# Eight convolution blocks and all of z multiplied from high and low weight halves, with memory's keys and values parked in DRAM, on one Trainium2 core

## The chip, the core and the metric

The kernel runs on one core of a Trainium2 chip. The core has five engines, each with its own in-order instruction stream: PE (TensorE, the matrix engine), DVE (VectorE), ACT (ScalarE), POOL (GpSimd) and SP (SyncE, which here only issues DMAs). They wait for each other through semaphores. The metric is the device time of one execution in microseconds (us); lower is better.

## What is computed

One step of a one-layer hybrid decoder on 320 tokens (256 of a prompt, 64 of eight samples), in 32-bit floats. Cut to the part that the change touches:

```python
def token_mixer(hn, ...):                   # hn: 320 tokens x 1024
    proj = hn @ w_in                        # z 1024, xbc 1536, dt 16, u5 1024, gates 2 x 1024
    z, xbc, dt_raw, u5, gate_a, gate_b = jnp.split(proj, IN_PROJ_SPLITS, axis=-1)
    xbc_c, new_conv = causal_depthwise_conv(xbc, conv_buf, conv_w, conv_b)   # 4 taps, then silu
    xs, bm, cm = jnp.split(xbc_c, [...], axis=-1)
    dt = softplus(dt_raw + ssd_dt_bias)
    y_ssd, new_ssd = ssd_chunked_scan(xh, dt, a, bm, cm, ssd_h0)             # 16 heads
    y_ssd = rms_norm((y_ssd + ssd_d * xh) * silu(z), ssd_norm_g)
    ...                                     # S5 branch, GLU, gates, w_mix_out
def memory_kv(mem, g, w_k, w_v):            # mem: 256 x 1024, keys and values are outputs too
    mn = rms_norm(mem, g)
    return mn @ w_k, mn @ w_v
...                                         # attention over memory, then 32 experts (192 MB of weights)
```

## The kernel before

The program has two parts. In the first some 650 us everything up to the experts' router is computed; PE is the busy engine. Then the experts' weights stream in, 1 MB chunks through a ring of places in on-chip memory, and DMA is busy without a break until near the end.

**Products.** A projection of 1024 inputs to 128 outputs for 320 tokens is one "job": eight matmuls of a stationary 128x128 tile of weights with a moving 128x320 tile of the normed input. `proj` (line 1310) does this on plain 32-bit floats; the profile shows each such matmul as two records. `proj_split` (lines 1667 to 1669) does it from halves: weights and input are each split into a high half (the value rounded to the reduced type that TensorE takes in fewer passes) and a low half (what is left), and three products are summed, high x high, high x low, low x high; each is one record. From job `ga0` on all projections are made this way, on "units" of 256 weight columns: ACT writes the high half (line 1006), DVE the low half (line 2419).

**Order.** `plan()` lists all jobs in the order in which PE does them, and gives each in turn one of six PSUM banks. PE waits with a job until the bank's job of six places earlier has been emptied. Every engine's stream is written out by hand in the same order of jobs, so what an engine waits for also holds back all that stands behind it. The stages that matter here:

- `STAGE`: memory's keys `mk0..7` (to `kT`) and values `mv0..3` (to `vm`), with the S5 branch's inputs between them. DVE runs the S5 scans (`scan`, `step_out`) meanwhile.
- `xbc0..11`, the convolution's input. For each, ACT copies the bank to a padded row `cvin` (`conv_in`, lines 878 and 879), DVE does the four taps into `cvout` (`conv`, lines 2222 to 2229), and ACT applies silu two blocks later (`conv_silu`, lines 885 and 888). `cvin` and `cvout` have two places each: `conv_in(m)` waits for `conv(m-2)`, and `conv(m)` waits for `conv_silu(m-2)`. The small jobs `dtT`, `dt3`, `cs` (time steps and their sums) stand after `xbc5`, `xbc7`, `xbc9`.
- `ye/yo/kk/fy/ty`, the S5 branch's outputs: `kk0` (line 1480) gives taps that DVE spreads to `kbd` (lines 2322 and 2330), `fy` (line 1491) uses them, `ty` needs ACT to have emptied `ye` and `yo`.
- `ko..`: the keys transposed back (line 1295) for their output; then `z0`, `z1`, `z2` by `proj` with small jobs between; `cumT`, `ecs`, `tr/tb/cb`.
- the heads: eight rounds t = 0..7 (`cs`, `yi`, `h0`, `yx`, `ns`). The five jobs `z3..7` are spread over it matmul by matmul (`rest_z`, line 1565): eight ahead of it, three in each round, eight behind it; then `hl`, then `ga0`.

**Weights.** Blocks of 512 columns (2 MB) go through two slots (`load_block`, line 532). SP loads a block when the last job of the block two before it is done: the second block of `xbc` when `mv3` is done, the third when `xbc3` is, the first of z (`z0..3`) when `xbc7` is, the second of z (`z4..7`) when `xbc11` is.

**Stores.** POOL issues them: values (`out_mv`, line 749) after `mv3`, keys (`out_mk`, line 751) after `ko`.

## Time and profile before

| what | value |
|---|---|
| median of three runs | 1124.7 us (1123.86 to 1130.07) |
| the profiled execution | 1127.23 us, of which its span is 1125.5 us |
| PE, DVE, ACT, POOL busy | 87%, 41%, 27%, 5% of the span |
| DMA | 297.69 MB, mean 265 GB/s |

The profile's page cuts the span in 40 slices of 28 us and gives each engine's busy tenths. Timeline rows give start, duration, engine, line, what is written from what, its size and how many instructions are merged; in brackets the idle time before it and who ended that. The duration of a merged row runs from its first start to its last end, and a matmul's end is modelled and overlaps the next one's start; so the time that a matmul costs is read from start to start. A row for a line alone may end with "DMA to landing", the time from a transfer's issue to its completion.

### The profile page before, as it was taken

The numbers are of one execution on the slowest core, as the hardware profiler recorded it, in microseconds if no ns is written. First come the engines' busy times: TensorE is split into PE (matmuls) and PEld (weight loads), VectorE is DVE, ScalarE is ACT, GpSimd is POOL, SyncE is SP. The second block draws the span as 40 slices with busy tenths as digits, with TensorE's granted clock in tenths as the row PEclk, the third lists the DMA queues.
The fourth block names the chain that finished last, engine by engine and source line by source line (L and its number), as shares of the span: only waits on it lengthen the run. The fifth ranks groups of instructions, "written<-read, shape, count | busy, mean of one in ns | idle before, by whom it ended". The sixth has DMA issues, their size and how long they took to land.

```text
span 1125.5 us, 15894 instructions
## 1 busy us (share of the span) xinstructions
PE 980.3 (87%) x6619; PEld 655.0 (58%) x6619; DVE 464.4 (41%) x795; ACT 305.3 (27%) x610; POOL 53.9 (5%) x82
## 2 busy tenths in 40 slices
PE   6999999999999999999898999976867768787575
PEld 4788467886779999999766954432222313232121
DVE  5999965405676554555455331020202020201014
ACT  4142124235546435544443341000000000000002
POOL 2602300010110000000000000000000000000000
PEclk9999999999999999999999999988898888788778
DMA  9581433023436574523578749999999999999994
GB/s 272 120 231 61 149 142 137 14 85 119 136 105 228 183 266 150 197 88 130 214 287 344 305 158 409 422 421 422 422 421 422 422 420 422 423 421 422 422 418 150
DMA packets 92435, 297.69 MB, mean 265 GB/s; under 512 B 21053, under 2 KB 31001, under 8 KB 68172
## 3 DMA queue, kind: packets, MB, share of 16 engines
q1 hardware_dynamic: 89812, 288.81, 67.0%
q0 software_dynamic: 2112, 7.28, 2.0%
q8 instruction: 53, 0.87, 0.3%
q10 hardware_dynamic: 440, 0.59, 0.2%
q14 instruction: 18, 0.15, 0.0%
HBM read 286.76 MB, written 9.90 MB: 264 GB/s over the span
## 4 chain that ended last, share of the span: by engine, by line
PE 61%; SPq 29%; DVE 4%; DMA 2%; issue 2%; ACT 1%; POOL 1%; DVEq 0%; ACTq 0%; POOLq 0%
SPq L629 29%; PE bank L1310 11%; PE bank L1295 6%; PE bank L1667 5%; PE bank L1668 5%; PE bank L1669 5%; PE bank L1954 3%; PE bank L1319 2%; DMA ring<-in_w_exp_down_dram 2%; PE bank L2003 2%; PE bank L1678 2%; PE bank L1565 2%; PE bank L1680 2%; PE bank L1679 2%; PE bank L1491 2%
## 5 line engine op out<-in xcount | busy, mean ns | idle before, releaser
L1954 PE MATMUL bank<-ring,work 128*32 128x512 f32 x704 | 134.9, 698 | 39.2 <-DMA ring<-in_w_exp_gate_dram 21.9
L1310 PE MATMUL bank<-work,ring 128*128 128x320 f32 (+1 forms) x480 | 125.6, 420 | 0.0
L1667 PE MATMUL bank<-ops,usplit 128*128 128x320 f32 x368 | 114.3, 311 | 1.1 <-DVE usplit L2419 1.1
L1668 PE MATMUL bank<-ops,usplit 128*128 128x320 f32 x368 | 114.0, 310 | 0.0
L1669 PE MATMUL bank<-ops,usplit 128*128 128x320 f32 x368 | 113.9, 310 | 0.0
L1310 PEld LDWEIGHTS bank<-work,ring 128*128 128x128 f32 x480 | 90.1, 190 | 30.7 <-issue 1.0
L1970 PE MATMUL bank<-ring,work 128*32 128x512 f32 x352 | 73.0, 822 | 39.0 <-DMA ring<-in_w_exp_down_dram 29.8
L1954 PE MATMUL bank<-work 128*32 128x512 f32 x256 | 87.1, 714 | 12.4 <-DMA work<-in_w_exp_up_dram 6.6
L2419 DVE TENSOR_TENSOR usplit<-ring,usplit 128x2048 fp32r<-128x2048 f32 x32 | 73.3, 2291 | 58.5 <-ACT usplit L1006 58.5
L1954 PEld LDWEIGHTS bank<-ring,work 128*32 128x32 f32 x704 | 32.4, 125 | 106.2 <-issue 86.9
L1006 ACT ACTIVATE usplit<-ring 128x2048 fp32r<-128x2048 f32 x32 | 61.4, 1919 | 52.7 <-PE bank L1669 36.7
L2718 DVE TENSOR_TENSOR work<-bank,g 128x512 f32<-128x512 f32 x8 | 5.5, 692 | 161.6 <-PE bank L2003 161.6
L1667 PEld LDWEIGHTS bank<-ops,usplit 128*128 128x128 f32 x368 | 69.2, 188 | 2.2 <-issue 2.0
L1669 PEld LDWEIGHTS bank<-ops,usplit 128*128 128x128 f32 x368 | 69.2, 188 | 0.0
L1668 PEld LDWEIGHTS bank<-ops,usplit 128*128 128x128 f32 x368 | 69.1, 188 | 0.1
L2003 PE MATMUL bank<-work 128*128 128x128 f32 (+1 forms) x384 | 68.7, 308 | 0.2 <-DVE work L2662 0.2
L2003 PEld LDWEIGHTS bank<-work 128*128 128x128 f32 (+1 forms) x384 | 52.3, 188 | 27.1 <-issue 13.3
L1970 PEld LDWEIGHTS bank<-ring,work 128*32 128x32 f32 x352 | 17.0, 145 | 82.0 <-issue 54.9
L2733 DVE COPY work<-bank 128x512 f32<-128x512 f32 x8 | 5.5, 692 | 124.0 <-PE bank L1970 124.0
L1678 PE MATMUL bank<-usplit,ops 128*128 128x256 f32 (+1 forms) x192 | 54.6, 285 | 1.7 <-DVE ops L2424 1.0
L1680 PE MATMUL bank<-usplit,ops 128*128 128x256 f32 (+1 forms) x192 | 53.9, 281 | 0.0
L1679 PE MATMUL bank<-usplit,ops 128*128 128x256 f32 (+1 forms) x192 | 53.9, 281 | 0.0
(461 smaller groups left out, 1555.7 us busy)
## 6 DMA issues: line engine op xcount, KB each, us to landing
ring<-in_w_exp_up_dram SPq DMA_DIRECT2D x45, 1024.0 KB, 26.1
ring<-in_w_exp_gate_dram SPq DMA_DIRECT2D x43, 1024.0 KB, 26.1
ring<-in_w_exp_down_dram SPq DMA_DIRECT2D x43, 1024.0 KB, 26.4
ring<-in_w_in_dram SPq DMA_DIRECT2D x11, 2048.0 KB, 8.8
work<-in_w_exp_gate_dram SPq DMA_DIRECT2D x16, 1024.0 KB, 21.7
work<-in_w_exp_up_dram SPq DMA_DIRECT2D x16, 1024.0 KB, 26.3
work<-in_w_exp_down_dram SPq DMA_DIRECT2D x14, 1024.0 KB, 26.7
ring<-in_w_glu_dram SPq DMA_DIRECT2D x4, 2048.0 KB, 8.7
```

The lines of the kernel that those rows point to most:

```text
L629: sp.dma_start(v, src).then_inc(sem_, 16)
L1310: ins = nc.tensor.matmul(b[:, 0:N], wv[:, k, P * (m % 4):P * (m % 4 + 1)], src[:, k, 0:N], start=(k == 0), stop=(k == KT - 1))
L1667: nc.tensor.matmul(b[:, 0:T], wh, hi_[:, k], start=(k == 0), stop=False)
L1668: nc.tensor.matmul(b[:, 0:T], wh, lo_[:, k], start=False, stop=False)
L1669: ins = nc.tensor.matmul(b[:, 0:T], wl, hi_[:, k], start=False, stop=(k == KT - 1))
L1678: nc.tensor.matmul(b[0:R, 0:256], th_, uhi[u % 2][:, k], start=(k == 0), stop=False)
L1679: nc.tensor.matmul(b[0:R, 0:256], th_, ulo[u % 2][:, k], start=False, stop=False)
L1680: ins = nc.tensor.matmul(b[0:R, 0:256], tl_, uhi[u % 2][:, k], start=False, stop=(k == KT - 1))
L1954: ins = nc.tensor.matmul(psum[part][ES * x:ES * (x + 1), :], xs[i % 2][:, kk, x], wt[x][:, k], start=(kk == 0), stop=(kk == KT - 1))
L1970: ins = nc.tensor.matmul(psum[2 + n_][ES * x:ES * (x + 1), :], hhT[:, j, x], wd[x][:, k, BLK * n_:BLK * (n_ + 1)], start=(j == 0), stop=(j ...
L2003: ins = nc.tensor.matmul(b[:, P * j:P * (j + 1)], tn[0:R, c, 4 * r_ + j], sel[i % 2][0:R, c].rearrange("p x n -> p (x n)"), start=(c == 0) ...
L2419: TT(ulo[u % 2], unit_raw(u), uhi[u % 2].bitcast(F32), ALU.subtract).then_inc(s["wlo"], 1)
```

## The change

- **Halves.** `xbc4..11` and `z0..7`, sixteen jobs, are multiplied as three products of halves. `HALVED` lists them in order, two halves (of four 128x128 tiles) each. ACT writes high half i to one of three places in `w_his` (`high_half`), when the products of half i-3 are done and the weight block is in; DVE writes the low half over the weights in their slot (`low_half`); `half_products` on PE waits for it. The four jobs `xbc0..3` (`WHOLE`) stay as they were.
- **z spread anew.** `z0`, `z1`, `z2` now stand between `xbc8`, `xbc9`, `xbc10` and `xbc11`; `z3` is made where it was; `z4..7` go as four pieces (each three matmuls) into each of the eight rounds of heads, and none is left behind them. `cs` moves from after `xbc9` to after `xbc11`.
- **The input's halves.** `hn_hi`, `hn_lo` are made before the convolution and no more at `ga0`. They and `w_his` lie where keys, values and `kout` were. So the `ko` jobs move between `mv0` and `mv1`; POOL stores keys and values and parks a copy of both in DRAM (`kv_scratch`, 1 MB each); ACT waits for the keys' store ahead of `hn_hi`, DVE for the values' store and copy ahead of `hn_lo`. After `gb7` POOL loads both back, and the attention waits for that.
- **Moves.** `cvin`, `cvout` and `dtS` lie where the memory input was; `ecs`, `btok`, `cbT`, `zT` have other places; `conv` of a block is interleaved with low halves on DVE, and three low halves (22 to 24) stand behind six `block_taps`; `hl` stands after `ga0`; unit 0's low half stands in the last round of heads; the silu of z is in two pieces.

When a block of weights is loaded is as before.

```diff
-LATE = {5: ["dtT"], 7: ["dt3"], 9: ["cs"]}
+LATE = {5: ["dtT"], 7: ["dt3"], 11: ["cs"]}
+WHOLE = [f"xbc{m}" for m in range(4)]
+HALVED = ([f"xbc{m}" for m in range(4, 8)] + ["xbc8", "z0", "xbc9", "z1", "xbc10", "z2", "xbc11"]
+          + [f"z{m}" for m in range(3, KT)])
+ROW = HALVED[:HALVED.index("z3")]
+HIS = 3
...
+        def half_left(eng, i):
+            job = HALVED[i // 2]
+            if i % 2 == 0:
+                eng.wait_ge(s["half_p"], i // 2 + 1)
+            elif job in BANK:
+                got(eng, job)
+            else:
+                eng.wait_ge(s["zf"], int(job[1:]) - 2)
...
             done(pool, "mv3")
-            pool.dma_start(o["mv"][0, 0].rearrange("(c p) a d -> p c (a d)", p=P), vm).then_inc(s["out_kv"], 16)
+            pool.dma_start(o["mv"][0, 0].rearrange("(c p) a d -> p c (a d)", p=P), vm).then_inc(s["out_mv"], 16)
+            pool.dma_start(kv_scr[:, 2048:4096], vm.rearrange("p c d -> p (c d)")).then_inc(s["sp_v"], 16)
...
+            def high_half(i):
+                name, high, _, raw_ = halves(i)
+                if i < HIS:
+                    act.wait_ge(s["sp_k"], 16)
+                else:
+                    half_left(act, i - HIS)
+                act.wait_ge(w_in_sem[BIDX[name] % STAT_SLOTS], loads(BIDX[name]))
+                act.activation(high, raw_, ACT.Copy).then_inc(s["bhi"], 1)
...
+            for job in WHOLE + ROW:
+                n_ = HALVED.index(job) if job in ROW else None
+                if job[0] == "z":
+                    keep_z(int(job[1:]))
+                else:
+                    m = int(job[3:])
+                    conv_in(m)
+                if n_ is not None:
+                    high_half(2 * n_ + 4)
+                if job[0] == "x":
...
+                    if m >= 2:
+                        conv_silu(m - 2)
...
+                if n_ is not None and job != ROW[-1]:
+                    high_half(2 * n_ + 5)
...
+            def half_products(b, i, k0, k1):
+                _, high, low, _ = halves(i)
+                if k0 == 0:
+                    pe.wait_ge(s["blo"], i + 1)
+                for k in range(k0, k1):
+                    kk = 4 * (i % 2) + k
+                    nc.tensor.matmul(b[:, 0:T], high[:, k], hn_hi[:, kk], start=(kk == 0), stop=False)
+                    nc.tensor.matmul(b[:, 0:T], high[:, k], hn_lo[:, kk], start=False, stop=False)
+                    ins = nc.tensor.matmul(b[:, 0:T], low[:, k], hn_hi[:, kk], start=False, stop=(kk == KT - 1))
...
+            dve.wait_ge(s["out_mv"], 16)
+            dve.wait_ge(s["sp_v"], 16)
+            for k in range(KT):
+                low("hn", (hn_hi, hn_lo), hnT, lambda x: x[:, k], k + 1)
+            conv(0)
+            conv(1)
+            low_half(0)
+            low_half(1)
+            for m in range(2, 6):
                 conv(m)
+                low_half(2 * m - 2)
+                low_half(2 * m - 1)
...
+            conv(10)
+            step_rates()
+            conv(11)
+            chunk_sums()
```

**DVE, between the S5 scans and the convolution.** `work` is the large buffer, L2284/L2285 clear the padding of `cvin`, L2222 to L2229 are one `conv`. Before:

```order
L2270 TENSOR_TENSOR ring<-ring,work 128x16x144 [waits dve]
L2284 MEMSET work 128x3
L2285 MEMSET work 128x3
L2222 COPY work<-early 128x8x3 [waits free2,dve]
L2224 TENSOR_SCALAR work<-work,vec 128x344 [waits dve]
L2226 SCALAR_TENSOR_TENSOR work<-work,vec 128x344 [waits dve] x3
L2228 COPY early<-work 128x3 [waits dve]
L2229 COPY early<-work 128x24
```

and now (L2375 is the low half of the input, L2301 to L2308 one `conv`, L2370 a low half of weights):

```order
L2349 TENSOR_TENSOR ring<-ring,work 128x16x144 [waits dve]
L2364 MEMSET work 128x3 [waits full5]
L2365 MEMSET work 128x3
L2375 TENSOR_TENSOR ops_52<-work,ops_57 128x320 [waits sp_v,hn_hi,out_mv,dve]
L2375 TENSOR_TENSOR ops_52<-work,ops_57 128x320 [waits hn_hi] x7
L2301 COPY work<-early 128x8x3 [waits free0]
...
L2301 COPY work<-early 128x8x3 [waits free1]
...
L2308 COPY early<-work 128x24
L2370 TENSOR_TENSOR wr_lo<-ring,w_his 128x4x128 [waits bhi] x2
L2301 COPY work<-early 128x8x3 [waits xc,free2]
```

What moved: eight instructions that wait for the stores `out_mv` and `sp_v` stand ahead of the first two `conv`, and these ahead of the first low halves, for which PE waits in `xbc4`.

**ACT, at the last block of the convolution.** L878/L879 are `conv_in`, L885/L888 `conv_silu`, L916 empties `ye0` and the like. Before, from `conv_in(11)`:

```order
L878 ACTIVATE work<-bank 128x256 [waits convout,full4]
L879 ACTIVATE work<-bank 128x8x8
L885 ACTIVATE work<-work 128x256 [waits convout]
L888 ACTIVATE work<-work 128x64
L885 ACTIVATE work<-work 128x256 [waits convout]
L888 ACTIVATE work<-work 128x64
L885 ACTIVATE work<-work 128x256 [waits convout]
L888 ACTIVATE work<-work 128x64
L916 ACTIVATE ring<-bank 40x32x16 [waits full5]
```

and now (L932/L933 `conv_in`, L920 `high_half`, L939/L942 `conv_silu`, L989 as L916; `w_slot0` is the semaphore of the slot into which the second z block is loaded):

```order
L932 ACTIVATE work<-bank 128x256 [waits convout,full4]
L933 ACTIVATE work<-bank 128x8x8
L920 ACTIVATE w_his<-ring 128x512 [waits w_slot0,full4]
L939 ACT_TABLE_LOAD
L939 ACTIVATE work<-work 128x256 [waits convout]
L942 ACTIVATE work<-work 128x64
L939 ACTIVATE work<-work 128x256 [waits convout]
L942 ACTIVATE work<-work 128x64
L939 ACTIVATE work<-work 128x256 [waits convout]
L942 ACTIVATE work<-work 128x64
L989 ACTIVATE ring<-bank 40x32x16 [waits full0]
```

What moved: between `conv_in(11)` and `conv_silu(9)` stands a high half of z's second block, and a table load.

## Rows read from the trace of the kernel before

**Rows 1.** The page's row of busy engines, and the DMA row of its 40 slices

```profile
PE 980.3 (87%) x6619; PEld 655.0 (58%) x6619; DVE 464.4 (41%) x795; ACT 305.3 (27%) x610; POOL 53.9 (5%) x82
...
DMA  9581433023436574523578749999999999999994
```

**Rows 2.** Waits of PE from 135 to 350 us: total, times, longest

```profile
PE bank L1626 <- DVE work L2382: 1.8, 1, 1.8
PE bank L1491 <- DVE ring L2330: 1.8, 1, 1.8
```

**Rows 3.** PE timeline: six blocks xbc0 to 5, ko, z0, z2

```profile
134.79 26.00 PE L1310 MATMUL bank<-work,ring 128*128 128x320 f32 x96
...
239.25 1.97 PE L1295 MATMUL bank<-ident,work 128*128 128x128 f32 x16
241.06 4.47 PE L1310 MATMUL bank<-work,ring 128*128 128x320 f32 x16
...
252.55 4.57 PE L1310 MATMUL bank<-work,ring 128*128 128x320 f32 x16
```

**Rows 4.** PE timeline of ga0: first products of tiles 2 and 19

```profile
336.16 0.31 PE L1667 MATMUL bank<-ops,usplit 128*128 128x320 f32 x1
...
343.64 0.31 PE L1667 MATMUL bank<-ops,usplit 128*128 128x320 f32 x1
```

**Rows 5.** PE timeline: pieces of rest_z in a round of heads, and the eight behind

```profile
276.31 0.70 PE L1565 MATMUL bank<-work,ring 128*128 128x320 f32 x2
276.85 0.38 PE L1635 MATMUL bank<-work,ring 128*128 128x128 f32 x2
...
330.32 4.66 PE L1565 MATMUL bank<-work,ring 128*128 128x320 f32 x16
```

**Rows 6.** DVE timeline: start and end of one conv, a copy-sized step of 512 columns, of 320

```profile
154.21 0.17 DVE L2222 COPY work<-early 128x24 f32<-128x24 f32 x1
...
156.82 0.17 DVE L2229 COPY early<-work 128x24 f32<-128x24 f32 x1
...
329.08 0.69 DVE L2414 TENSOR_TENSOR ring<-ring,bank 128x512 f32<-128x512 f32 x1
...
335.01 3.31 DVE L2424 TENSOR_TENSOR ops<-work,ops 128x320 fp32r<-128x320 f32 x8 [1.49 <-PE bank L1565]
```

**Rows 7.** ACT timeline: copies of 512 columns, a table load, copies of 320

```profile
239.95 2.07 ACT L931 ACTIVATE work<-bank 128x512 f32<-128x512 f32 x4 [0.77 <-PE bank L1295]
...
253.15 1.28 ACT L950 ACT_TABLE_LOAD   x1
...
330.56 2.99 ACT L1014 ACTIVATE ops<-work 128x320 fp32r<-128x320 f32 x8 [4.09 <-PE bank L1649]
```

**Rows 8.** Landing of three undisturbed 2 MB blocks, the values' store, the keys' store

```profile
DMA to landing us min/median/max: 7.6/7.6/8.6
...
out_mv_dram<-work POOLq DMA_DIRECT2D x1, 1024.0 KB, 10.3
out_mk_dram<-work POOLq DMA_DIRECT2D x1, 1024.0 KB, 4.4
```

**Rows 9.** PE and DVE timeline: kk0, its wait, the first fy, the fourth ye

```profile
194.52 2.02 PE L1480 MATMUL bank<-ring,work 128*32 128x128 f32 x64
...
198.35 2.86 PE L1491 MATMUL bank<-work,ring 128*128 128x320 f32 x16 [1.80 <-DVE ring L2330]
...
209.28 1.94 PE L1468 MATMUL bank<-ring,work 64*40 64x128 f32 x32 [0.20 <-DVE work L2337]
...
196.59 1.22 DVE L2322 TENSOR_TENSOR ring<-bank,sel 128x1024 f32<-128x1024 f32 x1 [1.74 <-PE bank L1480]
```

**Rows 10.** Windows: us, PE, PEld, DVE, ACT, POOL busy, PEclk, DMA share, GB/s

```profile
1062.00:1064.00 2.00, 0.00 (x0) 0.00 (x0) 0.00 (x0) 0.00 (x0) 0.00 (x0) 1.00 1.01 422
...
1066.00:1068.00 2.00, 1.71 (x9) 0.40 (x13) 0.00 (x0) 0.00 (x0) 0.00 (x0) 0.50 1.00 418
...
1070.00:1072.00 2.00, 2.00 (x16) 0.32 (x8) 0.00 (x0) 0.00 (x0) 0.00 (x0) 0.66 0.98 410
```

More of the change, by code:

```diff
@@ L151, in plan @@
     j += STAGE
-    for m in range(CT):
-        j += [f"xbc{m}"] + LATE.get(m, [])
+    for job in WHOLE + ROW:
+        j += [job] + (LATE.get(int(job[3:]), []) if job[0] == "x" else [])
     j += ["ye0", "yo0", "ye1", "yo1", "kk0"]
@@ L160, in plan @@
             j.append("kk1")
[L161 to L164 removed]
+    j += ["s5o0", "s5o1", "cumT"] + [f"nc{q}" for q in range(3)]
     j += [f"ecs{q}" for q in range(4)]
@@ L445, in op @@
             return view(ops[at][:, :], (KT, T))
-        hn_hi, hn_lo = op(18176), op(0)
+        hn_hi, hn_lo = op(18176), op(6656)
         yb_hi, yb_lo = op(9216), op(13056)
@@ L1413, in _ @@
                     proj("mk", m, mnT, MEM)
+                elif kind == "ko":
+                    b = take(job)
+                    done(pe, "mk7")
+                    for j in range(4):
+                        ins = tr(b[:, P * j:P * (j + 1)], kT[:, 4 * (m % 10) + j, P * (m // 10):P * (m // 10 + 1)])
+                    end(ins, job)
                 elif kind == "mv":
@@ L1431, in _ @@
             al = [ones[:, :], ones[:, :], same_s[:, :, :].rearrange("p b l -> p (b l)")]
-            for m in range(CT):
-                proj("xbc", m, hnT, T)
+            def half_products(b, i, k0, k1):
[7 more added lines that the diff above has]
+                    ins = nc.tensor.matmul(b[:, 0:T], low[:, k], hn_hi[:, kk], start=False, stop=(kk == KT - 1))
+                if i % 2 == 0 and k1 == 4:
+                    ins.then_inc(s["half_p"], 1)
+                return ins
+            for job in WHOLE + ROW:
+                m = int(job.lstrip("xbcz"))
+                if job in WHOLE:
+                    proj("xbc", m, hnT, T)
+                else:
+                    if job == ROW[0]:
+                        pe.wait_ge(s["hn_lo"], KT)
+                    b, n_ = take(job), HALVED.index(job)
+                    half_products(b, 2 * n_, 0, 4)
+                    end(half_products(b, 2 * n_ + 1, 0, 4), job)
+                if job[0] == "z":
+                    continue
                 if m == 5:
@@ L1544, in _ @@
             end(ins, "cumT")
-            proj("z", 2, hnT, T)
+            pe.wait_ge(s["convout"], CT)
+            for i in range(3):
+                b = take(f"nc{i}")
+                for j in range(4):
+                    ins = tr(b[0:27, P * j:P * (j + 1)], last3[:, 4 * i + j])
+                end(ins, f"nc{i}")
             done(pe, "cumT")
@@ L1699, in _ @@
                     end(nc.tensor.matmul(b[:, 0:T], ones[:, :], yr1, start=True, stop=True), "ssy")
-                proj_split("ga", m, hn_hi, hn_lo, "hn_lo" if m == 0 else None)
+                proj_split("ga", m, hn_hi, hn_lo)
+                if m == 0:
+                    done(pe, "s11")
+                    for i in range(2):
+                        b = take(f"hl{i}")
+                        for j in range(4):
+                            ins = tr(b[:, P * j:P * (j + 1)], hl[:, P * (4 * i + j):P * (4 * i + j + 1)])
+                        end(ins, f"hl{i}")
             for m in range(4):
```

262 lines of the change are left out of this document (139 added, 123 removed).

## The prediction

> **What bounds the kernel now.** I read the page first: PE is busy 87% of the span, and the DMA digits are low until slice 24 and 9 from there on [rows 1]. So there are two parts in a row: one that PE sets, and a stream of weights that can't start before the first is done, since its places come free with PE's work. A microsecond on PE's path ahead of slice 24 moves everything behind it by a microsecond. Second, PE's waits from 135 to 350 us: two of 1.8 us and little else [rows 2]. The stretch is PE without gaps, so fewer passes on PE are worth their full time, and every new gap costs its full length. Third, the timelines of PE, DVE and ACT there, for what one step costs.
>
> **What a block gains.** Six plain jobs take 134.79 to 160.72, 4.32 us each; z0 to z2 4.3 to 4.5 us [rows 3]. In `ga0` 17 tiles of three products take 336.16 to 343.64, 0.44 us a tile [rows 4], 3.52 us a job. So 0.80 us a job, and 16 jobs give 12.8 us, if nothing else changed. The Trainium skill ("FP8 and Floating Point Precision", TensorE Precision Notes) counts four passes for a true 32-bit product; three for four would be 3.24 us a job, and the sum below 4.5 us lower. The row says 3.52, and I keep the row.
>
> **A timetable of the new order.** I follow PE, DVE and ACT through it on the old profile's clock. Durations: one `conv` 2.72 us (154.21 to 156.9), a low half of 512 columns 0.69 alone and 0.60 in a chain, the input's eight low halves 3.31 [rows 6]; a high half 0.62 alone and 0.53 in a chain, a table load 1.28 [rows 7]; a block of weights 7.6 us from issue to landing, 7.7 with its wait [rows 8].
>
> *First gap.* The four `ko` jobs push `xbc0` to 136.9; `xbc3` ends at 154.2. DVE may not start the input's low halves before values are stored and copied. The store was issued 0.9 us after `mv3` and took 10.3 us beside the 2 MB block that is issued at the same moment; alone such a store takes 4.4, of which some 2.6 move data [rows 8]. So: 136.9 + 0.9 + 10.3 + 2.6 for the copy behind it = 150.7, I take 151. Bounds: 147 (the copy wholly beside the store) and 153 (4.4 behind it). Then DVE: 3.3, two `conv` 5.4, one low half 0.7: `xbc4` can start at 160.4. PE idles 6.2 us. Queued behind DVE's wait are all `conv`, and behind these ACT's `conv_in(2)`.
>
> *The clock.* After idle windows late in the trace PE comes back at 1066.3 with a granted clock of 0.50, its 1.2 GHz level; the mean of 0.66 in the window from 1070 says that it was back at 2.4 GHz by about 1071.4 [rows 10]. At half rate for 5 us, PE loses about 2.5; I charge 2.35 us after each gap of over 4 us, bounds 0 and 2.5.
>
> *Second gap.* From there PE is the later one: DVE needs 2.72 + 1.2 = 3.9 us a block against PE's 3.52, but started ahead. `xbc4` ends at 166.3; four jobs, `dtT` and `dt3` (1.9 together) end `xbc8` at 182.3, `xbc7` at 178.1. But z's first block is loaded only when `xbc7` is done, and `z0` now stands one job behind it; before, it had a lead of 70 us. 178.1 + 7.7 + 0.62 + 0.69 = 187.1: PE idles 4.8 us, plus the clock. ACT waits for this block ahead of `conv_silu(5)`, DVE ahead of `conv(7)`, but both catch up, since two of five following jobs have no `conv`. `xbc11` ends at 187.1 + 5.9 + 5 x 3.52 = 210.6.
>
> *Third gap.* This one is read from ACT's order at the last block. Behind `conv_in(11)` ACT makes a high half of z's second block, which SP loads when `xbc11` is done: 210.6 + 7.7 = 218.3. Behind it, in line, stand the table load and `conv_silu(9)`; `conv(11)` on DVE waits for that one's place in `cvout`; `block_taps(0)` stands behind `conv(11)`; and `fy0` on PE waits for the taps. So 218.3 + 0.5 + 1.28 + 0.57 = 220.6, `conv(11)` 2.7, sums 0.5, first taps 1.6: `fy0` starts at 225.5. PE has `cs` 1.3, four `ye/yo` 3.6 and `kk0` 2.0 to do after `xbc11`, to 217.5, and idles 8.0 us; before this place cost 1.8 [rows 9]. With the clock `fy0` ends at 230.6. Then `ty0`, `ye2/yo2`, `kk1` to 235.2, two taps, three low halves and the first output on DVE, and the fourth `ye` starts at 240.5 instead of 209.28 [rows 9]: 31.2 us late.
>
> *What comes back.* `ko`, `z0`, `z1`, `z2` are gone behind it: 1.8 + 4.3 + 4.3 + 4.5 = 14.9 [rows 3]. `z3`: eight tiles of 0.56 become about 0.48: 0.6. The heads are PE's to the last: a piece costs 0.54 from start to start where nothing has to switch, up to 0.7 where it does, 15.2 for 24, and the eight behind them 4.5 [rows 5], 19.7 in all; after, 32 tiles of 0.44 and half a microsecond for switches a round, 17.1: 2.6 back. Their added work on DVE and ACT, 0.6 and 0.5 us a round of 7, is covered by idle time there, which every round has. Two squeezes cost: `ecs` waits for ACT, whose table load lost its cover (z2, 4.5 us), 1.1; and at `ga4` DVE's unit 2 comes behind a silu that begins only after `hl`, 1.3 (each between 0 and 2). `hn_hi` and `hn_lo` leave `ga0`: nothing on PE's path there before.
>
> **Hidden edits.** Storing and parking keys falls in a stretch with no other transfer but one block that has 6 us to spare. Loading both back, 2 MB after `gb7`, delays one weight block by some 5 us; blocks there are 14 us of PE each against 7.7 of landing, and the attention is 100 us away. If that cover were gone it would cost up to 5.
>
> **Sum.** +31.2 - 14.9 - 0.6 - 2.6 + 1.1 + 1.3 = +15.5. The profiled execution took 1127.23 us for its span of 1125.5, the median is 1124.7. The profiled sum would be 1142.7; against the median 1140.2.
>
> **Rivals.**
>
> (a) *The gaps come, but the clock stays up.* For it: in the stretch from 135 to 350 us PE never sat idle long enough to show. Against: rows 10. Three times 2.35 would be 7; after the first two gaps part of it hides behind waits for low halves, so 5 in all comes off: +10, 1135. The Trainium skill ("TensorE: Matmul & The Clock Gate", Part 1) has the clock fall to 1.2 GHz after idleness and return with work, which agrees with rows 10 and speaks for the forecast.
>
> (b) *The third gap isn't there*: ACT's wait holds nobody up, because `conv(11)` has its place or the block lands early. Then `fy0` waits as before, and the sum is 8.7 us lower: +7, 1131.5. Against it: the rule `conv(m)` after `conv_silu(m-2)` stands in both kernels, and the block's load is tied to `xbc11`.
>
> (c) *Much shorter landings*: values out by 146, as with nothing beside them, and blocks in 5 us, the time that their bytes moved. First gap 1, second 2, third 5, no clock: about +1, 1126, no change.
>
> (d) *Faster.* DVE and ACT run far enough ahead that all three gaps are covered. It decides at the first gap: values stored and copied by 144.7 (7 us after `mv3`'s eviction), and the others at a landing of under 3 us. Then only the jobs count: 12.8 less 0 to 3 for squeezes, 1113. Against it: no landing of 2 MB under 7.6 in this trace [rows 8].
>
> **Numbers.** Forecast 0.55, (a) 0.20, (b) 0.11, (c) 0.09, (d) 0.05. A measurement of this kernel tells about 0.5%, 5.6 us, from no change. Slower: the first three and a little of (c), 0.87; same 0.08; faster 0.05. Range: down to (b) with a first gap that starts at 147, 31.2 - 8.7 - 4 - 15.7 = about +3, 1128; up to 153 for the store, both squeezes at 2, the reload uncovered: +15.5 + 2 + 1.6 + 2 = +21, 1146.
>
> **What would show it.** Right: PE waits of some 6 us at the first product of `xbc4`, released by DVE's low half; some 5 at `z0`, where ACT's high half waits for a DMA; some 8 at the first `fy`, released by the taps, with DVE idle about 10 us ahead of `conv(11)`; a granted clock of 0.50 behind them; the end of `ga0` 10 to 16 us later, and the rest of the trace shifted alike. Wrong: jobs of another length than 3.5 us; a first low half before 155; `conv(11)` right behind `step_rates`; waits of PE in the heads, which I have at none; or a stream whose length changes.

## The result, and the profile after

The changed kernel takes 1152.66 us (median of four executions, 1149.86 to 1160.70) beside 1127.38 for the kernel before (1123.86 to 1133.57): a ratio of 1.0223 [1.0178, 1.0269]. The forecast was 1140.2, slower by 15.5 us; it is slower by 25.3, and 1152.66 lies above the range, which ended at 1146. Measured once more later, beside the experiments, the same kernel took 1148.68 and the kernel before 1132.42 (1.0168 [1.0115, 1.0221], 16.3 us). Of the 9.0 us between the two differences 4.0 lie in the changed kernel and 5.0 in the kernel before, whose own median moved from 1127.38 to 1132.42.

The page of the profiled execution (it took 1160.70 us, the longest of the four), the rows that answer to [rows 1] and the clock by slices:

```profile
span 1159.0 us, 16267 instructions
PE 989.1 (85%) x6747; PEld 681.8 (59%) x6747; DVE 483.6 (42%) x827; ACT 322.4 (28%) x643; POOL 55.6 (5%) x85
...
PEclk9999988899959999999999999999898888788788
DMA  9482632203434376453368876999999999999994
```

The span grew by 33.5 us. PE is busy 8.8 us longer though 12.8 us of work at full clock were taken out: slice 12 of the clock's row, about 319 to 348 us, has a 5. The waits of PE from 135 to 380 us, total, times and longest, stand against the two of [rows 2]:

```profile
PE bank L1504 <- DVE wr_lo L2370: 11.0, 2, 6.0
PE bank L1580 <- DVE ring L2448: 9.5, 1, 9.5
PE bank L1557 <- DVE work L2455: 2.1, 1, 2.1
PE bank L1703 <- DVE work L2504: 1.8, 1, 1.8
PE bank L1354 <- ACT ring L1014: 1.0, 1, 1.0
PE bank L1670 <- ACT ring L1053: 0.7, 3, 0.2
```

L1504 is the first of the three reduced products of a tile, L1580 the chunk sum (`fy`), L1557 the state product (`ye`), L1354 a transpose, L1703 the head products `yi`, L1670 the decays. The three gaps and what ends them, from the timelines of PE, DVE and ACT (start, us, engine, line; in brackets the idle time ahead):

```profile
149.73 3.31 DVE L2375 TENSOR_TENSOR ops<-work,ops 128x320 fp32r<-128x320 f32 x8 [9.59 <-DMA kv_scratch<-work]
...
159.19 0.61 PE L1504 MATMUL bank<-ops,w_his 128*128 128x320 f32 x1 [6.02 <-DVE wr_lo L2370]
...
184.22 0.63 ACT L920 ACTIVATE w_his<-ring 128x512 fp32r<-128x512 f32 x1 [7.24 <-DMA ring<-in_w_in_dram]
...
185.72 0.61 PE L1504 MATMUL bank<-ops,w_his 128*128 128x320 f32 x1 [4.99 <-DVE wr_lo L2370]
...
217.54 0.63 ACT L920 ACTIVATE w_his<-ring 128x512 fp32r<-128x512 f32 x1 [8.06 <-DMA ring<-in_w_in_dram]
...
220.14 0.18 DVE L2301 COPY work<-early 128x24 f32<-128x24 f32 x1 [11.41 <-ACT work L942]
...
225.20 5.47 PE L1580 MATMUL bank<-work,ring 128*128 128x320 f32 x16 [9.48 <-DVE ring L2448]
...
240.71 0.56 PE L1557 MATMUL bank<-ring,work 64*40 64x128 f32 x6 [2.08 <-DVE work L2455]
```

And the windows (PE busy is the first number behind the length, the granted clock the third from the end):

```profile
156.00:162.00 6.00, 2.81 (x11) 2.84 (x12) 5.72 (x13) 3.46 (x10) 0.00 (x0) 0.50 0.74 282
...
184.00:188.00 4.00, 2.28 (x9) 2.31 (x10) 2.73 (x6) 2.95 (x9) 0.00 (x0) 0.50 0.00 0
...
222.00:230.00 8.00, 4.80 (x14) 4.06 (x15) 7.37 (x17) 2.49 (x6) 0.00 (x0) 0.50 0.00 0
...
320.00:344.00 24.00, 24.00 (x105) 19.24 (x103) 7.21 (x17) 6.45 (x18) 0.89 (x1) 0.50 0.24 70
```

The first three are the half clock (1.2 of 2.4 GHz) behind a gap. The fourth isn't: for 24 us PE's row is busy without a break, and it runs at half clock (in all for some 31 us, from 316 to 347). It lies in the heads. Their eight rounds, by the start of `yi` on PE:

```profile
292.98 0.92 PE L1703 MATMUL bank<-work,ring 128*64 128x128 f32 x12 [1.79 <-DVE work L2504]
...
300.77 0.92 PE L1703 MATMUL bank<-work,ring 128*64 128x128 f32 x12
...
316.47 1.53 PE L1703 MATMUL bank<-work,ring 128*64 128x128 f32 x12
...
330.05 1.53 PE L1703 MATMUL bank<-work,ring 128*64 128x128 f32 x12
...
343.29 1.53 PE L1703 MATMUL bank<-work,ring 128*64 128x128 f32 x12
...
351.64 0.92 PE L1703 MATMUL bank<-work,ring 128*64 128x128 f32 x12
```

A round takes 7.79 us at full clock (6.61 or 7.14 before); the fourth and fifth take 13.58 and 13.24, the last two 8.35 and 6.74. Divided at two places that both kernels have, the first product `s0` and the first gate product (`ga0`), the 33.5 us lie like this:

| stretch | before | after | again | change |
|---|---|---|---|---|
| to `s0` | 268.6 | 287.7 | 289.1 | +19.1 |
| `s0` to `ga0` (heads) | 67.0 | 79.6 | 68.1 | +12.6 |
| `ga0` to the end | 789.9 | 791.7 | 792.3 | +1.8 |

"Again" is the profile of the second measurement. It has the same three waits, and only one short fall of the clock in the heads. A small part of the work changes stretch: the transposes of `hl`, 0.8 us (334.81 to 335.65 before), stood in the second and now stand in the third. The last stretch differs by 3.7 us at most between all profiles of this study, so what happens ahead of `ga0` is the whole matter.

### The profile page after: what moved, and what is told of

The parts are those of the page before. It is cut to its first block, busy times and chain, and to the rows that moved or that the text cites. A ratio compares the mean times of both kernels' runs of the same rounds, so it can differ in the third digit from the quotient of the medians.

```text
span 1159.0 us, 16267 instructions
## 1 busy us (share of the span) xinstructions
PE 989.1 (85%) x6747; PEld 681.8 (59%) x6747; DVE 483.6 (42%) x827; ACT 322.4 (28%) x643; POOL 55.6 (5%) x85
## 4 chain that ended last, share of the span: by engine, by line
PE 56%; SPq 28%; DVE 5%; DMA 5%; ACT 3%; issue 2%; POOL 1%; DVEq 0%; ACTq 0%; POOLq 0%
SPq L656 28%; PE bank L1354 6%; PE bank L1369 5%; PE bank L1738 4%; PE bank L1739 4%; PE bank L1740 4%; PE bank L2033 3%; PE bank L1378 2%; DMA ring<-in_w_exp_down_dram 2%; PE bank L2082 2%; PE bank L1504 2%; PE bank L1749 2%; PE bank L1750 2%; PE bank L1751 2%; PE bank L1580 2%
## 5 line engine op out<-in xcount | busy, mean ns | idle before, releaser
L2033 PE MATMUL bank<-ring,work 128*32 128x512 f32 x704 | 134.2, 695 | 39.6 <-DMA ring<-in_w_exp_gate_dram 22.5
L2049 PE MATMUL bank<-ring,work 128*32 128x512 f32 x352 | 71.2, 807 | 40.3 <-DMA ring<-in_w_exp_down_dram 32.5
L1369 PE MATMUL bank<-work,ring 128*128 128x320 f32 (+1 forms) x304 | 76.9, 411 | 0.0
L1369 PEld LDWEIGHTS bank<-work,ring 128*128 128x128 f32 x304 | 57.1, 190 | 17.1 <-issue 0.5
L2049 PEld LDWEIGHTS bank<-ring,work 128*32 128x32 f32 x352 | 16.7, 142 | 82.0 <-issue 53.2
L1749 PE MATMUL bank<-usplit,ops 128*128 128x256 f32 (+1 forms) x192 | 54.6, 284 | 1.7 <-DVE ops L2375 1.0
L1504 PE MATMUL bank<-ops,w_his 128*128 128x320 f32 x128 | 46.6, 364 | 11.0 <-DVE wr_lo L2370 11.0
L1751 PE MATMUL bank<-usplit,ops 128*128 128x256 f32 (+1 forms) x192 | 53.9, 281 | 0.0
```

Source lines behind the costliest of these rows:

```text
L1369: ins = nc.tensor.matmul(b[:, 0:N], wv[:, k, P * (m % 4):P * (m % 4 + 1)], src[:, k, 0:N], start=(k == 0), stop=(k == KT - 1))
L1504: nc.tensor.matmul(b[:, 0:T], high[:, k], hn_hi[:, kk], start=(kk == 0), stop=False)
L1749: nc.tensor.matmul(b[0:R, 0:256], th_, uhi[u % 2][:, k], start=(k == 0), stop=False)
L1751: ins = nc.tensor.matmul(b[0:R, 0:256], tl_, uhi[u % 2][:, k], start=False, stop=(k == KT - 1))
L2033: ins = nc.tensor.matmul(psum[part][ES * x:ES * (x + 1), :], xs[i % 2][:, kk, x], wt[x][:, k], start=(kk == 0), stop=(kk == KT - 1))
L2049: ins = nc.tensor.matmul(psum[2 + n_][ES * x:ES * (x + 1), :], hhT[:, j, x], wd[x][:, k, BLK * n_:BLK * (n_ + 1)], start=(j == 0), stop=(j ...
```

## The experiments

Two questions: are the gaps what the prediction says, and what happens in the heads? "The stretch" below is `s0` to `ga0`; its times and every clock are from the run's one profile. The runs were made in four groups, with the kernel before measured anew beside each; its medians were 1132.4, 1132.6, 1129.7 and 1132.4. "The repeat" is the first run, of the first group.

### The changed kernel again

> The changed kernel once more, unchanged, beside the runs below. Theory that its loss in the heads (the stretch from the product s0 to the product s1, 76.8 us in its first profile, 58.4 before) is part of the change: the profile again shows three waits of PE of about 6.0, 5.0 and 9.5 us, and again a stretch of the heads at a granted clock of 0.50 in which PE waits for nothing; the ratio to the kernel before is again 1.018 to 1.027. Rival, that the clock in the heads is chance of one execution: the three waits stand, the heads run at 1.00 and take some 60 to 62 us.

1148.68 us (1147.7 to 1151.3). Waits of 5.7, 5.1 and 10.2 us; the stretch 68.1. In it rounds of 7.79, 7.79, 7.79, 8.42, 9.89, 6.74, 6.74 and one clock window under 1.00 (0.57 from 324 to 332). So the fall in the heads is there again, at the same round, but lasts some 7 us in place of 31. The long one belongs to some executions, not to all; neither theory as written fits.

### The high half behind the Silu

```
             for job in WHOLE + ROW:
...
-                if n_ is not None:
+                if n_ is not None and job != ROW[-1]:
                     high_half(2 * n_ + 4)
...
             conv_silu(CT - 1)
+            high_half(2 * len(ROW) + 2)
```

> ACT's high half of z's fourth block (half 24, which waits for z's second weight block) stands behind the last three groups of the convolution's Silu instead of ahead of them; nothing else is moved. Theory of the prediction: the third gap goes, the wait at the first chunk sum falls from 9.5 to 1.8 to 2.2 us, the clock does not fall to 0.50 behind it, the fourth state product (ye3) starts 8.7 us earlier and the whole ends 8 to 9 us earlier. Rival, that the chain to the first chunk sum is bound by DVE's convolutions and not by the landing: the wait stays over 6 us and the gain is under 3 us. Rival, that the heads' half clock hangs on the gaps ahead of them: the heads run at 1.00 and the gain is 20 us or more.

1142.41 us. The wait at the first chunk sum is as before the change (PE timeline):

```profile
219.03 2.86 PE L1581 MATMUL bank<-work,ring 128*128 128x320 f32 x16 [1.81 <-DVE ring L2449]
```

`s0` comes 10.3 us earlier than in the repeat, and the profiled span is 8.6 us shorter (1140.9 for 1149.5), against the 8.7 of rival (b); the medians are 6.3 us apart, less than the 8 to 9 expected. The wait is gone with the one move. That settles the third gap: it was one instruction, waiting for a DMA ahead of three others that did not need it. Of the 10.3 us 1.8 were given back in the heads (69.8 for 68.1), where the clock fell three times for a moment (0.79 in 284 to 292, 300 to 308 and 316 to 324). Taking the gap away did not keep the clock up there.

### z0 to z2 later

```
-["xbc8", "z0", "xbc9", "z1", "xbc10", "z2", "xbc11"]
+["xbc8", "xbc9", "xbc10", "z0", "z1", "z2", "xbc11"]
```

(from the line of `HALVED`; DVE's loop follows it).

> z's first three jobs stand later in the row of the projection: xbc8, xbc9, xbc10, z0, z1, z2, xbc11 in place of xbc8, z0, xbc9, z1, xbc10, z2, xbc11, with DVE's low halves and convolutions in the same order; nothing else. Theory of the prediction: z0 waited 5.0 us only for the landing of z's first weight block, which starts when xbc7 is done; two jobs of 3.52 us more ahead of it cover 7.0 us, so the second gap is gone with the half clock behind it, and xbc11 is done 7.3 us earlier. What comes back: the landing of z's second block starts with xbc11's end as before, so the third gap stays at 9 to 10 us and the whole ends 6 to 7.5 us below the changed kernel. Rival, that the wait of z0 is the chain of halves on ACT and DVE: a wait of over 2 us stays at z0 and the gain is under 4 us.

1142.38 us, 6.3 below the repeat. Waits of PE:

```profile
PE bank L1580 <- DVE ring L2447: 8.8, 1, 8.8
PE bank L1504 <- DVE wr_lo L2370: 6.8, 5, 6.1
```

Of 10.8 us at L1504 6.8 are left, 6.1 of them the first gap. The third gap stays, at 8.8 us (9 to 10 were expected), and `s0` comes 7.0 us earlier. The second gap was the wait for the landing of z's first block: with the landing covered, 0.7 us in four waits is left at this line.

### Six whole blocks

```
-WHOLE = [f"xbc{m}" for m in range(4)]
+WHOLE = [f"xbc{m}" for m in range(6)]
```

(`HALVED` begins with `xbc6`, and the numbers of the halves on ACT and DVE follow it; DVE does `conv(2)` and `conv(3)` ahead of the first low half.)

> Six blocks of the convolution's input are made of whole f32 products in place of four, so that six and not eight stand in halves ahead of z; nothing else. Theory of the prediction: the first gap (6.0 us ahead of the fifth block, for the store and the copy of the values that DVE's low part waits for) is covered by two blocks of 4.32 us and goes with the half clock behind it: minus 6.0 and minus about 2.3, plus 2 times 0.80 for the blocks that are whole again, so xbc7 is done 6.7 us earlier; the second and third waits stand as they are, and the whole ends 6 to 7 us below the changed kernel. Rival, that the copies land late for another reason that moves with PE: a wait of over 2 us stays ahead of the seventh block, and the gain is under 3 us.

1157.34 us (1148.4 to 1160.2). The first gap shrank only to 2.4 us, since in this order DVE does the third and fourth convolution ahead of the first low half, and the one at `z0` stays at 5.1. `s0` is 4.2 us earlier where 6.7 were expected. The whole was expected 6 to 7 us below the changed kernel and is 8.7 above the repeat: the clock is at 0.50 from 316 to 344 in the heads, with rounds of 13.58 and 13.24 us, the same lengths as in the first profile of the changed kernel. Three of its four executions lie at 1157 to 1160 and one at 1148.4, as a long and a short fall would have it; only one of them is profiled.

### The heads' order

ACT's timeline in a round of the changed kernel:

```profile
306.56 0.63 ACT L920 ACTIVATE w_his<-ring 128x512 fp32r<-128x512 f32 x1 [3.45 <-PE bank L1506]
307.10 1.07 ACT L1053 ACTIVATE ring<-bank 128x512 f32<-128x512 f32 x2
308.63 1.55 ACT L1029 ACTIVATE work<-bank,early 128x128 f32<-128x128 f32 x6 [0.47 <-PE bank L1670]
```

The high half (L920) waits for PE's last piece of the round, for the place it writes to. The two evictions of old states (L1053) stand behind it, PE's decays (L1670) need the banks that these free, and so PE starts its decays late in every round that has a high half. The edit puts it at the end:

```
             for t in range(KT):
-                high_half(26 + t)
                 if t:
                     got(act, f"yx{t - 1}")
...
                     rest_z(t // 2 + 3)
+                high_half(26 + t)
```

and DVE's low half behind the round's output.

> In the heads ACT makes its high half behind the two evictions of old states and the decays of its round instead of ahead of them, and DVE its low half later to match. Theory order: the high half ahead of the evictions is what made the first four rounds 7.8 us instead of 6.9 and thinned PE's row until the clock fell; the 0.24 us waits of the decays for ACT are gone, rounds take 6.9 to 7.1 us at clock 1.00 throughout, the heads 58 to 60 us, and the time is 12 to 18 us below the changed kernel. Theory pieces: what lowers the clock is that PE now works on three products in the reduced type where it had one in f32, whatever the order; the rounds at 1.00 are shorter by 0.3 to 0.8 us, the clock still falls to 0.50 without a wait in the middle of the heads, and the time is 2 to 6 us below the changed kernel.

1143.79 us, 4.9 below the repeat; the waits at L1670 are gone, rounds at full clock take 6.74 or 7.28, the stretch 64.3. But it has rounds of 8.25 and 8.93 with clocks of 0.80 and 0.78 (300 to 316), and one of four executions took 1153.1. So both theories hold a part: the order is worth about 4.2 us (five rounds of 7.79 against 34.8 in the version with three fixes below), and the clock falls without it too. By the time, 4.9 us for the 12 to 18 of theory order and the 2 to 6 of theory pieces, it is the second. ACT's and DVE's halves were moved together; that ACT's was the one that cost is read from the timeline and from the waits at L1670.

### Plain pieces in the heads

> z's last five blocks are made of whole f32 pieces again, four in a round, with ACT's and DVE's halves for them left out; their right side is the rounded part of the normed input alone, so what the low part of the input would add to these five blocks is left out of the result. Since no half waits for z's second block any more, the wait of 9.5 us at the first chunk sum (the third gap) is gone too: 1.5 to 2.5 us stay there, and about 8.7 us less is expected from that under every theory. Theory order: as the high halves are gone from the heads, rounds are 6.6 to 7.1 us at 1.00 as before, some 24 us less in all. Theory pieces: the same, since the f32 pieces are back: the heads at 1.00, 57 to 60 us. Rival, that the clock falls in the heads because of the gaps and the half clock before them and not for anything in the heads: the clock falls to 0.50 here too, and the gain is the 8.7 us alone.

1131.95 us, ten executions within 1130.1 to 1133.4. The wait at the first chunk sum is 1.8, the stretch 64.4 with every clock window at 1.00, rounds of 7.14 to 7.68. That is longer than expected (from `s0` to `s1` 62.8 us, for 57 to 60), since a round now has four f32 pieces where it had three before. It is 16.7 us below the repeat and level with the kernel before (1.0005 [0.9976, 1.0034]), with two gaps of 11.0 us together still in it; 24 us less had been expected. The rival, that the gaps ahead lower the clock in the heads, falls here.

### The kernel before with lighter heads

```
                 for n in range(n0, n1):
                     m, k = 3 + n // KT, n % KT
+                    if k < KT - 1:
+                        continue
```

> The kernel before with 35 of the 40 f32 pieces of z's last five blocks left out (each block is one product of its last slice of 128 rows, so z3 to z7 are wrong); all else is as before. It asks what lowers the clock in the heads. Theory activity: the f32 pieces were what kept TensorE busy enough; without them the granted clock falls to 0.50 for one or more stretches of 3 us and over between s0 and the first gate product although PE waits for nothing long, and rounds there lengthen. Theory kind: it is the reduced type of the new pieces; without any pieces the heads run at 1.00 throughout, in rounds of 5.2 to 5.6 us, and s0 to s1 takes 44 to 48 us in place of 58.4. Both: about 16.2 us less PE work (35 times 0.463), of which DVE's row may give back some.

This is the run that says most. 16 us of PE work less (by the expectation's 0.463 a piece; 19 by the 0.54 of [rows 3]), and it takes 1138.80 us, 6 more than the kernel before (1.0068 [1.0029, 1.0106]). The stretch takes 81.3 us in place of 67.0. Windows of this run:

```profile
276.00:284.00 8.00, 8.00 (x44) 6.38 (x40) 4.25 (x9) 2.96 (x10) 0.94 (x1) 0.53 0.27 74
284.00:292.00 8.00, 8.00 (x34) 5.29 (x35) 4.61 (x10) 3.36 (x10) 0.90 (x1) 0.50 0.42 121
292.00:300.00 8.00, 8.00 (x53) 6.68 (x51) 4.61 (x10) 3.68 (x11) 0.89 (x1) 0.71 0.37 106
300.00:308.00 8.00, 8.00 (x37) 5.64 (x38) 3.69 (x9) 3.06 (x10) 0.89 (x1) 0.50 0.33 94
```

and of the kernel before:

```profile
276.00:284.00 8.00, 8.00 (x65) 6.25 (x63) 4.45 (x10) 3.36 (x10) 0.94 (x1) 1.00 0.02 7
284.00:292.00 8.00, 8.00 (x62) 6.04 (x61) 5.24 (x12) 3.36 (x10) 0.90 (x1) 1.00 0.64 185
```

PE is at 8.00 busy in both. What differs is what it is busy with: products of 8 columns, of 32 rows, transposes of 128, with or without three pieces of 128x320 among them in a round. At 0.50 these small ones take nearly twice as long (eight transposes 1.76 us from start to start, 0.93 at 1.00), and the row of busy time shows nothing of it. In the round from 277.68 the start-to-start time of every group is some 1.9 times that at 1.00, so no wait is hidden in the row either. The clock's first fall here (0.54 and 0.60 from 266 to 270) does follow waits, of 0.8 and 1.6 us; after it the clock is back at 1.00 from 270 to 276, and what falls from then on follows no listed wait but one of 0.4. So in this kernel the clock hangs on what PE does, not only on whether it is busy, and z's pieces were what held it.

The Trainium skill ("TensorE: Matmul & The Clock Gate", Part 4) says of transposes that they don't count as PE-busy for the clock gate the same way. These windows agree in direction: eight transposes of 128x128 stand in a round beside the small products. Which of these kinds counts how much, no run here tells apart. The Trainium skill's advice on the same page ("Why this matters for your kernels"), to leave no long idle gap between matmuls, would have the clock stay up in this run, whose longest wait of PE from 262 us on is 1.6 us; the measurement decides against it as a full rule.

### Filler in the heads of the changed kernel

```
                     b = take(f"yi{t}")
+                    for _ in range(2):
+                        nc.tensor.matmul(b[:, 0:T], ident[:, :], xcT[:, t], start=True, stop=True)
```

(six products of `hn_hi` with itself in the second run).

> The changed kernel with two added f32 products of 128x320 in each of the eight rounds of the heads, written into the bank of the round's result ahead of the products that start it anew, so that the result is untouched: 16 products of 0.46 us, 7.4 us more PE work. Theory activity (from the kernel before with its f32 pieces left out, which fell to half clock through most of the heads): the added work keeps the clock: no fall between s0 and the first gate product, s0 to the first gate product 71 to 73 us against 68.1, and its runs lie within 3 us of each other where the changed kernel's lay up to 11 apart. Rival, that the fall is set by a time or by what lies ahead of the heads: the fall stays and s0 to the first gate product takes 75 us or more.

> The same with six added products of the reduced type (128x320, 0.147 us each in the row of the projection, 3.52 us for 24) in place of the two in f32: 0.88 us a round, 7.0 us in all, about the same PE time. Theory activity: as with the f32 products, the clock stays at 1.00 and s0 to the first gate product is 71 to 73 us. Theory kind, that products of the reduced type do not count toward the clock as those in f32 do: the clock still falls for 5 us or more somewhere in the heads, and the stretch takes 75 us or more.

1158.79 and 1159.08 us; the stretch 80.0 and 77.0. A round at full clock grew from 7.79 to 9.06 and 8.87, 10.2 and 8.6 us in eight, and the fall at 324 stayed in both (0.66 and 0.60 in the window from 324 to 332, with further windows of 0.79 and 0.88). The theory of activity missed in both: here added work did not hold the clock, whichever type it had. Both rivals came out by their numbers. That the f32 filler fails too speaks against the second one (kind); the first one (what lies ahead) is tried in the next run. In both, ACT's high half still keeps the decays waiting.

### Order and filler together

> The changed kernel with the heads' order mended (high halves behind the evictions) and one added f32 product of 128x320 in each round of the heads (result untouched); the three gaps ahead of the heads stand. Theory activity, that the heads' own work decides: no fall of the clock from the product s0 to the first gate product, rounds of 7.5 and 8.0 us, the stretch 66 to 67 us, and runs within 5 us of each other, at 1144 to 1149 us. Rival, that the half clock behind the gaps ahead of the heads brings on the falls in them: one or two falls as without the filler, the stretch 69 us or more, runs 8 us or more apart.

1147.29 us, four executions within 1147.2 to 1149.3. The heads' windows (all three gaps are still ahead of them):

```profile
288.00:320.00 32.00, 31.11 (x234) 24.22 (x233) 21.28 (x46) 20.52 (x62) 2.72 (x3) 1.00 0.43 137
320.00:352.00 32.00, 32.00 (x247) 25.62 (x246) 20.05 (x41) 12.49 (x29) 3.54 (x4) 1.00 0.38 112
```

Rounds 7.48 and 8.02, the stretch 66.2. So with PE not held up in the round, and one f32 product of 320 columns more in each, this profile stays at 2.4 GHz, after the same gaps. What lies ahead is not enough to bring on the falls. It gains nothing: the filler costs 0.74 us a round (0.46 was expected), 5.1 us in the stretch against the 61.1 of the versions below, where the short falls without it cost 3.2 (64.3); the median is 3.5 us above that of the version without filler.

### The fixes together

> The three fixes without the six whole blocks: z0 to z2 later, the high half of z's fourth block behind the Silu, the high halves of the heads behind the evictions; four whole blocks as in the changed kernel. The first gap stands: 5.7 to 6.1 us ahead of the fifth block and a clock of 0.50 for some 5 us behind it; no other wait over 2.4 us up to the heads. Theory: relative to the version with six whole blocks it loses that gap and its half clock (8.3 us, less the 2.4 us that stayed there and twice 0.80 us of jobs in halves), so 3 to 5 us slower than that one. Rival, that the half clock behind a gap is paid back because the waiting engines catch up: within 2 us.

> The three moves and the order of the heads together: six whole blocks, z0 to z2 later, the high half of z's fourth block behind the Silu, the high halves of the heads behind the evictions. Theory of the prediction with the heads' order as found: no wait of over 2.2 us between the first and the last projection of the row, minus 6.7, minus 7.3, minus 8.7 and minus 6 in the heads, so 1118 to 1123 us, 0.5 to 1% below the kernel before. Rival, that the clock falls in other places once the gaps are gone (the heads with their reduced products above all): 1124 to 1132 us, no better than before.

> The version with all four edits and one added f32 product of 128x320 in each round of the heads (0.46 us each, 3.7 us in all; the result is untouched). Theory activity: the falls of the clock in the heads that its twelve runs of 1119.9 to 1141.7 us let guess are gone, the fastest runs are 3 to 4 us slower (1123 to 1125), the slowest much nearer to them (under 1132), and the median is within 2 us of the version without it. Rival, that the spread comes from stages far behind the heads: the spread stays at some 20 us and the median rises by 3.7 us.

> The version with four whole blocks, z0 to z2 later and no high half ahead of the Silu, with z's last five blocks from whole f32 pieces (32 in the eight rounds, 4 a round) in place of the pieces of three reduced products; what the low part of the input would add to these five blocks is left out. Against the version with the reduced pieces only the kind of product in the heads differs, and ACT's and DVE's halves there. Theory kind, that three reduced products (2.22 us for four pieces) keep the clock less well than f32 pieces (1.85 us for four) in the same places: its runs lie within 5 us of each other where the other's ten lay 16 apart, at 1123 to 1128 us, and the heads show no fall. Rival, that the spread of the other is chance or comes from behind the heads: single runs above 1134 us here too.

| run | us | executions | `s0` | stretch | ratio to before |
|---|---|---|---|---|---|
| three fixes | 1127.08 | 10, 1123.6 to 1139.4 | 271.5 | 61.1 | 0.9987 [0.9946, 1.0029] |
| with six whole | 1127.34 | 12, 1119.9 to 1141.7 | 269.7 | 61.1 | 0.9989 [0.9950, 1.0028] |
| and filler | 1129.30 | 12, 1127.7 to 1132.4 | 270.6 | 66.2 | 0.9992 [0.9963, 1.0021] |
| three fixes, plain pieces | 1128.23 | 10, 1126.4 to 1130.9 | 269.8 | 66.1 | 0.9964 [0.9930, 0.9997] |

The waits of the version with six whole blocks, up to the heads, show what is left of the three gaps:

```profile
PE bank L1505 <- DVE wr_lo L2371: 3.0, 4, 2.5
PE bank L1558 <- DVE work L2455: 2.4, 1, 2.4
PE bank L1581 <- DVE ring L2448: 1.8, 1, 1.8
```

The three fixes take back 21.6 us of the repeat's 1148.68. Six whole blocks for four bring 1.8 us at `s0` and 2.7 in the span, less than the 3 to 5 expected, and nothing in the median, as the rival had it. With all fixes 1118 to 1123 us had been expected; 1127.34 is in the range of that run's rival.

The filler cut the spread from 21.8 to 4.8 us, plain pieces from 15.8 to 4.5, and either took the fastest executions away with the slowest. With the filler the fastest execution is 1127.7, not the 1123 to 1125 expected, the slowest 1132.4, and the median 2.0 above the version without it. Both kinds of heavier round are steady, both light ones are not; nor is the kernel before, which has three plain pieces a round where the last version has four (14 to 19 us in the groups).

The last row is from another group than the first, so this pair is compared across groups; its highest execution, 1130.9, speaks against the rival that asked for some above 1134. That the scattered executions have the clock's falls in their heads is inferred from this and not shown: the profiled ones of both light versions show a clock of 1.00 throughout the heads, and it is the last version's that has a window of 0.79, from 276 to 284, where none had been expected.

No version here is faster than the kernel before by more than the 0.5% that can be told; the last one comes nearest and leaves a part of the sum out.

## Why the prediction was right, and where it failed

**What a block gains**, 3.52 us a job: right. Once the clock is back, at 163 us, the products of `xbc4` come 0.147 us apart, and 24 of them are 3.53.

**First gap**: expected at 160.4 with 6.2 us idle; 159.19 and 6.02. DVE was released at 149.73 for 151. Its cause was not taken away by itself; covering it with two whole blocks cut it to 2.4.

**Second gap**: expected at 187.1 with 4.8; 185.72 and 4.99, and gone when `z0` stands later.

**Third gap**: expected at 225.5 with 8.0; 225.20 and 9.48. Undoing one line took 8.6 us off the profiled span where 8.7 had been said (6.3 between medians).

**The clock behind the gaps**: 0.50 behind each, as forecast. Rival (a) is out. Behind the first gap PE works at half rate from 159.19 to 162.53, which costs 1.7 us, not 2.35; behind the third 5.4 us, 2.7.

**The sum up to the fourth `ye`**: +31.2 expected, +31.4 measured (240.71 for 209.28). That it fits to 0.2 is in part luck: `xbc11` ends at 208.9 for 210.6, and the third gap is 1.5 us longer, with a landing that ends 8.7 us after `xbc11` where 7.7 had been taken.

**What comes back**: up to `s0` the sum says 31.2 - 14.9 - 0.6 + 1.1 = +16.8, and it is +19.1 (in the second profile +20.5). Of the 2.3 missed, 1.7 are a fall of the clock that was not in it (some 3.4 us at half rate from 240 on), behind the wait of 2.1 us at the fourth `ye`. The squeeze at `ecs`, 1.1 in the sum, is there with 1.0: the transpose at 278.20 waits for ACT, whose evictions of `ecs` stand behind the table load.

**The heads**: the step that failed. It says 2.6 us back, "their added work on DVE and ACT ... is covered by idle time there, which every round has", and that a wait of PE in the heads would prove it wrong. Two things are wrong in it. The work of ACT was counted, its place was not: L920 waits for PE ahead of two evictions that PE waits for, and a round takes 7.79 in place of some 6.95, 4.2 us in five rounds, though PE's listed waits there are 0.7 us in all (the rest is in the decays' late start, with PE's row filled). And the clock was charged to idle gaps alone: it fell in the heads with PE's row full.

With the order mended and no fall the stretch takes 61.1 us against 67.0, 5.9 back. Of these 1.7 are the fall in the kernel before's own heads (0.79 from 324 to 332) and 0.8 is `hl`, which only moved behind `ga0`; so the pieces themselves gain 3.4, and the version with plain pieces in the same places, also without a fall, takes 3.3 more (64.4 for 61.1). The prediction has 2.6, and its own terms, 32 tiles of 0.44 and 8 times 0.5, add to 18.1 and not to 17.1, which would be 1.6. In the first profile 61.1 and 4.2 for the order leave 14.3 for the clock; in the second 2.8.

Set against the forecast, with `hl` moved, the two profiles miss it like this (us; the profiled spans are 33.5 and 24.0 above the kernel before's, for 15.5):

| stretch | forecast | first profile | second profile |
|---|---|---|---|
| to `s0` | +16.8 | +19.1 | +20.5 |
| heads | -3.4 | +12.6 | +1.0 |
| `ga0` to the end | +2.1 | +1.8 | +2.4 |

So the heads hold 16.0 of the 18.0 us missed in the first and 4.5 of 8.5 in the second. That the second measurement's difference of medians, 16.3, is so near to the forecast's 15.5 is luck: the kernel before had a median 5.0 us higher in it than in the first, and the profile of the second misses the forecast by 8.5 us.

**The range** had no term for the heads above -2.6 and so ended at 1146. A rival was missing: that lighter work on PE lowers its clock. The lighter heads show this in the kernel before; why the clock falls where it does in the changed kernel, and for how long, stays open: two fillers did not hold it there, a smaller one with the order mended did.

**The rest of the trace** is shifted alike, as forecast: 1.8 us from `ga0` on, of which 0.8 is `hl`; so 1.0 for the 1.3 in the sum.

## What to carry to other kernels

Where a change makes PE's work lighter in a stretch of small products (few columns, few rows, transposes), ask what held the clock there: taking out 16 us of work made one kernel 6 us slower. An instruction that waits for a transfer or for a place, put ahead of others in an engine's queue, costs by what is queued behind it and who waits for that; both errors found here were such an instruction of ACT, one ahead of the third gap and one in each of the rounds of heads, and moving it cost nothing that these runs show. PE's busy time doesn't show the second; the start-to-start time of a repeated round, beside its clock, does.

## What was not expected of the hardware

- The granted clock falls to 0.50 with PE at 8.00 busy in 8.00 us, for some 7 us in one execution and some 31 in another of the same kernel, beginning in the same round (the fourth). Why there, and why so differently long, is open.
- With two or three f32 pieces of 128x320 fewer in each round of heads, 0.50 to 0.71 in all windows of 8 us from 276 to 340 (the lighter heads); with one f32 product more a round and the order mended, 1.00 throughout and executions within 2.2 us. No difference between f32 filler and filler of the reduced type was found (80.0 and 77.0 us, the fall at the same place in both). Executions with four plain pieces a round are steadier than those with four of three reduced products in the same places (4.5 us for 15.8), but that was seen only together with ACT's and DVE's halves taken out.
- The kernel before spreads over 1122 to 1141 us itself. Its one profile shows a single short fall in the heads; where its longer executions lose their time is not shown, since each kernel has one profile.
